# First two projection chunks interleaved in pairs of weight blocks; memory pieces and cross-attention heads turned by transfers, moves of x issued from GpSimd

## What is computed

```python
h = rmsnorm(x, g_mix_pre); proj = h @ w_in             # 2048 x 7168
cb, cc, cv, dq, dk, dv, xq = split(proj)
y_conv  = (cb * causal_dwconv(cc * cv, conv_w)) @ w_conv_out
y_diff  = diff_attention(dq, dk, dv, ...) @ w_diff_out     # 8 heads
k, v    = split(rmsnorm(mem, g_mem) @ w_mem_kv)            # 256 memory tokens
y_cross = (softmax(xq k^T / 16) v) @ w_cross_out           # 4 heads of 256
gates   = sigmoid(h @ w_gate + b_gate)
x = x + rmsnorm((g_a*y_conv + g_b*y_diff + g_c*y_cross) @ w_o, g_mix_post)
u = causal_dwconv(rmsnorm(x, g_ffn_pre) @ w_up, ffn_conv_w)
x = x + rmsnorm((silu(gate) * val) @ w_down, g_ffn_post)
```

## Time and profile before

| | us |
|---|---|
| median of three runs | 1647.38 (1647.07 to 1651.2) |
| profiled execution, its own time | 1648.04 |
| its span, first to last instruction | 1646.3 |
| TensorE busy, whole span | 1634.2 (7301 matmuls) |
| VectorE / ScalarE / GpSimd busy | 1008.9 / 832.4 / 22.7 |
| VectorE: low parts of weight blocks | 690.2 (567 of 1.224) |
| ScalarE: high parts of weight blocks | 597.2 (567 of 1.059) |
| data moved by the 16 DMA engines | 345.13 MB, mean 210 GB/s |

### The profile page before, as it was taken

One profiled execution on the slowest core, in us unless ns is written; L12 is line 12 of the kernel. 1 busy time (PEld: TensorE's weight loads), 2 busy tenths in 40 slices (PEclk: granted clock), 3 DMA queues, 4 the chain that ended last, 5 costly groups with the idle time before them and its releaser, 6 DMA issues.

```text
span 1646.3 us, 22261 instructions
## 1 busy us (share of the span) xinstructions
PE 1634.2 (99%) x7301; PEld 1349.0 (82%) x7301; DVE 1008.9 (61%) x1342; ACT 832.4 (51%) x1056; POOL 22.7 (1%) x53
## 2 busy tenths in 40 slices
PE   9999999999999999999999999999999999999998
PEld 7788888888888888888888888888888888888886
DVE  5565556655566666666655757776766677744544
ACT  6654444444444444444444656666566655543442
POOL 0000000000000000000000000000000000000000
PEclk9999999999999999999999999999999999999999
DMA  7777666777666766676656477777777776755654
GB/s 266 249 220 242 181 174 181 230 215 220 194 198 196 238 207 210 197 235 209 226 197 222 135 227 204 221 219 215 215 222 218 217 220 213 243 192 167 217 193 139
DMA packets 204967, 345.13 MB, mean 210 GB/s; under 512 B 27672, under 2 KB 50537, under 8 KB 204393
## 3 DMA queue, kind: packets, MB, share of 16 engines
q1 hardware_dynamic: 201801, 343.53, 66.9%
q10 hardware_dynamic: 3104, 0.80, 0.2%
HBM read 318.02 MB, written 2.10 MB: 194 GB/s over the span
## 4 chain that ended last, share of the span: by engine, by line
PE 96%; DMA 1%; SPq 1%; DVE 1%; ACT 1%; issue 0%; POOL 0%; DVEq 0%; ACTq 0%; POOLq 0%
PE PS L1408 28%; PE PS L1409 27%; PE PS L1410 27%; PE PS L1535 3%; PE PS L1537 3%; PE PS L1536 3%; PE PS L1573 1%; PE PS L1571 1%; PE PS L1572 1%; DMA raw<-in_w_mem_kv_dram 1%; SPq L334 1%; PE PS L1474 0%; PE PS L1489 0%; DVE w_lo L935 0%; ACT w_hi L578 0%
## 5 line engine op out<-in xcount | busy, mean ns | idle before, releaser
L935 DVE TENSOR_TENSOR w_lo<-raw,w_hi 128x1024 fp32r<-128x1024 f32 x567 | 690.2, 1224 | 562.7 <-ACT w_hi L578 561.4
L578 ACT ACTIVATE w_hi<-raw 128x1024 fp32r<-128x1024 f32 x567 | 597.2, 1059 | 625.8 <-PE PS L1410 529.1
L1408 PE MATMUL PS<-w_hi,hT_hi 128*128 128x512 f32 x1504 | 588.0, 391 | 0.7 <-DVE w_lo L935 0.7
L1410 PE MATMUL PS<-w_hi,hT_lo 128*128 128x512 f32 x1504 | 585.3, 389 | 0.0
L1409 PE MATMUL PS<-w_lo,hT_hi 128*128 128x512 f32 x1504 | 585.2, 389 | 0.0
L1408 PEld LDWEIGHTS PS<-w_hi,hT_hi 128*128 128x128 f32 x1504 | 282.3, 188 | 62.0 <-issue 3.8
L1410 PEld LDWEIGHTS PS<-w_hi,hT_lo 128*128 128x128 f32 x1504 | 282.3, 188 | 59.1
L1409 PEld LDWEIGHTS PS<-w_lo,hT_hi 128*128 128x128 f32 x1504 | 282.3, 188 | 57.9
L1408 PE MATMUL PS<-w_hi,act_hi 128*128 128x512 f32 x336 | 130.9, 390 | 0.0
L1410 PE MATMUL PS<-w_hi,act_lo 128*128 128x512 f32 x336 | 130.7, 389 | 0.0
L1409 PE MATMUL PS<-w_lo,act_hi 128*128 128x512 f32 x336 | 130.7, 389 | 0.0
(11 more groups left out here) (218 smaller groups left out, 1258.3 us busy)
## 6 DMA issues: line engine op xcount, KB each, us to landing
raw<-in_w_up_dram SPq DMA_DIRECT2D x176, 512.0 KB, 4.0
raw<-in_w_in_dram SPq DMA_DIRECT2D x112, 512.0 KB, 4.2
raw<-in_w_gate_dram SPq DMA_DIRECT2D x96, 512.0 KB, 4.5
raw<-in_w_down_dram SPq DMA_DIRECT2D x88, 512.0 KB, 4.1
raw<-in_w_mem_kv_dram SPq DMA_DIRECT2D x32, 512.0 KB, 5.0
raw<-in_w_o_dram SPq DMA_DIRECT2D x32, 512.0 KB, 3.6
up_moved<-up_stage SPq DMA_DIRECT2D x352, 32.0 KB, 2.8
raw<-in_w_conv_out_dram SPq DMA_DIRECT2D x16, 512.0 KB, 3.7
```

The lines of the kernel that those rows point to most:

```text
L578: nc.scalar.activation(w_hi[i % RING][:], raw[i % RING][:], ACT.Copy).then_inc(hi_ready, inc)
L935: nc.vector.tensor_tensor(w_lo[i % RING][:], raw[i % RING][:], w_hi[i % RING][:].bitcast(F32), ALU.subtract).then_inc(lo_ready, inc)
L1408: nc.tensor.matmul(o, a_hi, b_hi, start=first, stop=False)
L1410: last = nc.tensor.matmul(o, a_lo, b_hi, start=False, stop=last_k)
```

## The change

- The blocks of the first two chunks (both memory values) are taken in pairs: blocks 0, 1 of chunk 0, blocks 0, 1 of chunk 1, blocks 2, 3 of chunk 0, and so on. Both accumulators are open at once. Chunk 0 is taken out at step 16 of ScalarE, not 11.
- TensorE turns memory pieces 0 and 1 only. Pieces 2 and 3 are turned like x: ScalarE's copy, 16 transfers, VectorE's transposes. Steps of the six pieces: `COPY_AT`, `TURN_AT`, `HI_AT`, `LO_AT`.
- The 96 transfers for these six pieces are issued by GpSimd (`move_piece`), with the mean square of memory between the second and the third piece. SyncE issues none of them.
- Loads of memory pieces 2 and 3 stand at steps 3 and 4 of SyncE, the constants' at step 6. The sums of squares of memory stand at ScalarE's steps 8 and 10, the constants' copies at VectorE's step 10.
- Cross heads: VectorE writes the normalised probabilities in squares (four instructions), 16 transfers exchange them (eight issued by ScalarE, at its step 7 and step 0 of the next chunk; eight by SyncE at steps 4 and 5 of the next chunk), VectorE transposes inside the squares at step 4 of the next chunk (four instructions), and TensorE multiplies with the values after its block 5 of that chunk, into bank 7. High and low parts follow at step 1 of the chunk after. TensorE's transposes and ScalarE's copy of the turned probabilities are gone.

The diff, cut to its core:

```diff
-    X_COPY = [8, 13, 18, 23]
+    PAIRED = [(c, KB * p + r) for p in range(NCH) for c in range(2) for r in range(KB)]
+    PIECES = [("mem", 2), ("mem", 3)] + [("x", g) for g in range(NCH)]
+    COPY_AT = [3, 5, 10, 14, 18, 22]
+    TURN_AT = [8, 11, 17, 21, 25, 29]
+    HI_AT = [9, 12, 18, 22, 26, 30]
+    LO_AT = [9, 12, 19, 23, 27, 31]
...
+        def chunk_block(c, i):
+
+            return PAIRED[c * CB + i] if c < 2 else (c, i)
...
-            def move_x(g, a):
-
-                if a == 0:
-                    sp.wait_ge(x_copied, g + 1)
-                    if g >= 2:
-                        sp.wait_ge(prep_turned, NCH + g - 1)
+            def move_cross(h, a):
+
+                if a == 2:
+                    sp.wait_ge(x_norm, h + 1)
+                    if h:
+                        sp.wait_ge(x_pT, h)
                 for m in range(P // SQ):
-                    sp.dma_start(x_moved[g % 2][SQ * m:SQ * (m + 1), a, :, :].rearrange("p q n -> p (q n)"),
-                                 x_stage[g % 2][SQ * a:SQ * (a + 1), m, :, :, :].rearrange("p b t n -> p (b t n)")).then_inc(x_moved_in[g % 2], 16)
+                    sp.dma_start(p_moved[SQ * m:SQ * (m + 1), a, :, :].rearrange("p q n -> p (q n)"),
+                                 p_stage[SQ * a:SQ * (a + 1), m, :, :].rearrange("p q n -> p (q n)")).then_inc(x_pT_in, 16)
...
-                        load(c * CB, i, w_mem_kv, i * KB, CROSS + half * CW)
+                        cc, kb = chunk_block(c, i)
+                        load(c * CB, i, w_mem_kv, kb * KB, CROSS + proj[cc][1] * CW)
...
-                    elif c == 0 and i < NCH:
-                        mem_columns(i * CW, (i + 1) * CW, mem_in[i])
-                    for g in range(NCH):
-                        if 0 <= c * CB + i - X_COPY[g] - 5 < P // SQ:
-                            move_x(g, c * CB + i - X_COPY[g] - 5)
...
+                    if 0 <= c - 1 - CROSS_STEP < CH and i in (4, 5):
+                        move_cross(c - 1 - CROSS_STEP, i - 2)
...
-                    if c == 0 and i == NCH + 1:
+                    if c == 0 and i == NCH + 2:
...
+            def move_piece(e):
+
+                pool.wait_ge(x_copied, e + 1)
+                if e >= 2:
+                    pool.wait_ge(prep_turned, 2 + e - 1)
+                for a in range(P // SQ):
+                    for m in range(P // SQ):
+                        pool.dma_start(x_moved[e % 2][SQ * m:SQ * (m + 1), a, :, :].rearrange("p q n -> p (q n)"),
+                                       x_stage[e % 2][SQ * a:SQ * (a + 1), m, :, :, :].rearrange("p b t n -> p (b t n)")).then_inc(x_moved_in[e % 2], 16)
+
+            move_piece(0)
+            move_piece(1)
             pool.wait_ge(squares, 2)
             rms(r_mem[:], sq_mem[:], D)
+            for e in range(2, len(PIECES)):
+                move_piece(e)
...
-                n_end = (c + 1) * CB
+                n_end = (c + 1) * CB + (CB - KB if c == 0 else 0)
...
+                    if c == 2 and i == 0:
+                        after_projection(0)
+                    if i == 3 and c >= 2:
                         after_projection(c - 1)
...
+                    if c * CB + i in COPY_AT:
+                        e = COPY_AT.index(c * CB + i)
+                        what, g = PIECES[e]
+                        act.wait_ge((mem_in if what == "mem" else x_in)[g], 16)
+                        if e >= 2:
+                            act.wait_ge(x_moved_in[e % 2], MOVED * (e // 2))
...
+                    if c == 0 and i == 3:
+                        prepare(1, 1, SCORE_T, gmem_v, memT_hi)
+                    if c == 1 and i in (0, 2):
+                        row_squares(i // 2, mem_sb, sq_mem, i // 2)
+                    if c * CB + i in HI_AT:
+                        e = HI_AT.index(c * CB + i)
...
-                            act.wait_ge(x_pT, h + 1)
-                            nc.scalar.activation(p_crossT[:], PS[:, 7, :].rearrange("p (a b) -> p a b", a=NT), ACT.Copy).then_inc(x_pT_sb, 1)
-                        if i == 7:
-                            act.wait_ge(x_oT, h + 1)
-                            nc.scalar.activation(y_cross_hi[:, 2 * h:2 * h + 2, :],
-                                                 PS[:, 6, :].rearrange("p (a b) -> p a b", a=2), ACT.Copy).then_inc(x_hi, 1)
+                            act.wait_ge(x_norm, h + 1)
+                            if h:
+                                act.wait_ge(x_pT, h)
+                            move_cross(h, 0)
+                    h = c - CROSS_STEP - 1
+                    if 0 <= h < CH:
+                        if i == 0:
+                            move_cross(h, 1)
+                    h = c - CROSS_STEP - 2
+                    if 0 <= h < CH and i == 1:
+                        act.wait_ge(x_oT, h + 1)
+                        nc.scalar.activation(y_cross_hi[:, 2 * h:2 * h + 2, :],
+                                             PS[:, 7, :].rearrange("p (a b) -> p a b", a=2), ACT.Copy).then_inc(x_hi, 1)
...
+                    if c * CB + i in TURN_AT:
+                        e = TURN_AT.index(c * CB + i)
+                        dve.wait_ge(x_moved_in[e % 2], MOVED * (e // 2 + 1))
+                        if e:
+                            dve.wait_ge(prep_lo, 2 * (2 + e))
...
+                                for kb in range(NT):
+                                    last = nc.vector.tensor_scalar(p_stage[:, :, NT * t + kb, :],
+                                                                   p_cross[:, t, kb * P:(kb + 1) * P].rearrange("p (m n) -> p m n", n=SQ),
+                                                                   inv_e[:, 0, t:t + 1], None, ALU.mult)
...
+                    h = c - CROSS_STEP - 1
+                    if 0 <= h < CH:
+                        if i == 4:
+                            dve.wait_ge(x_pT_in, MOVED * (h + 1))
+                            if h:
+                                dve.wait_ge(x_oT, h)
+                            for t in range(NT):
+                                for kb in range(NT):
+                                    last = nc.vector.transpose(p_crossT[:, kb, t * P:(t + 1) * P].rearrange("p (a n) -> p a n", n=SQ),
+                                                               p_moved[:, :, NT * t + kb, :])
+                            last.then_inc(x_pT, 1)
+                    h = c - CROSS_STEP - 2
+                    if 0 <= h < CH and i == 1:
+                        dve.wait_ge(x_hi, h + 1)
...
-                acc = ACC[c % 2]
+                    cc, kb = chunk_block(c, i)
+                    acc = ACC[cc % 2]
+                    if c < 2 or c == NCH:
+                        pe.wait_ge(prep_lo, (0 if c < 2 else 2 * NCH) + kb + 1)
+                    multiply(c * CB, i, CB, memT_hi if on_mem else hT_hi, memT_lo if on_mem else hT_lo, lambda t: acc[:, t, :], kb=kb)
                     if c == 1 and i == 2:
                         pe.wait_ge(const_ready, 3)
-                    if c == 0 and i in (0, 1, 3):
-                        turn_memory((0, 1, 3).index(i) + 1)
+                    if c == 0 and i == 1:
+                        turn_memory(1)
                     if c == 0 and i == CB - 1:
...
-                                pe.wait_ge(x_lo, h)
+                                pe.wait_ge(x_exp, h)
...
-                        if i == 3:
-                            pe.wait_ge(x_norm, h + 1)
+                    h = c - CROSS_STEP - 1
+                    if 0 <= h < CH and i == 5:
+                        pe.wait_ge(x_pT, h + 1)
+                        if h:
+                            pe.wait_ge(x_lo, h)
+                        for db in range(2):
                             for kb in range(NT):
-                                for t in range(NT):
-                                    last = nc.tensor.transpose(PS[:, 7, kb * TOK + t * P:kb * TOK + (t + 1) * P],
-                                                               p_cross[:, t, kb * P:(kb + 1) * P], ident[:])
-                            last.then_inc(x_pT, 1)
-                        if i == 4:
-                            pe.wait_ge(x_pT_sb, h + 1)
-                            for db in range(2):
-                                for kb in range(NT):
-                                    v0 = h * CHD + db * P
-                                    last = nc.tensor.matmul(PS[:, 6, db * TOK:(db + 1) * TOK], mv_tok[:, kb, v0:v0 + P],
-                                                            p_crossT[:, kb, :], start=kb == 0, stop=kb == NT - 1)
-                            last.then_inc(x_oT, 1)
+                                v0 = h * CHD + db * P
+                                last = nc.tensor.matmul(PS[:, 7, db * TOK:(db + 1) * TOK], mv_tok[:, kb, v0:v0 + P],
+                                                        p_crossT[:, kb, :], start=kb == 0, stop=kb == NT - 1)
+                        last.then_inc(x_oT, 1)
```

(26 more changed lines are left out.)

51 lines of the change are left out of this document (11 added, 40 removed).

## The result

The changed kernel takes 1651.17 us (median of 12 runs, 1649.02 to 1652.29); the kernel before took 1648.30 on the same chips (12 runs, 1647.07 to 1651.2). The ratio is 1.0016, 95% interval 1.0009 to 1.0024: 0.16% slower, where 0.33% faster was forecast. The profiled execution took 1651.51, its span 1649.7, 3.4 longer than before.

A forecast was written before the change was run, and what follows sets the result against it. TensorE was taken as the bound. 1648.04 - 1.77 - 1.78 - 2.24 + 0.4 = 1642.65 us, then 0.66 less for the median of earlier runs, gave 1642.0 (0.33% faster); range 1641.0 to 1657.

The forecast's parts named there:

- Bound and views: Whole kernel: TensorE busy 1634.2 of 1646.3 us; time comes only from work taken off it and from its few waits.
- Part 1: Start of the projection loop: memory pieces two and three no longer turned on TensorE, 1.77 us off.
- Part 2: Cross heads: probabilities turned by transfers instead of TensorE transposes, 0.445 us for each of four heads, 1.78 off.
- Part 3: Three TensorE stalls between 64 and 110 us, laid to SyncE's queue of x moves, counted gone whole: 2.24 us off.
- Part 4: First 16 blocks of two chunks interleaved: zero price on TensorE, only due times of memory pieces and chunk 0's evacuation move.
- Part 5: GpSimd issues 96 moves at a taken 0.615 us each: nothing waits, but 0.4 us allowed for piece 2 at block 8.
- signs of being wrong: Profile after: the prediction is wrong if p exceeds 0.73 or starts around the removed transposes lie no closer than before.
- p: GpSimd's time to issue one move, shown by no row before; taken as 0.615 us from SyncE's issue of the same moves.
- Part 6: Cross-head work put on ScalarE, SyncE and VectorE: inside 5.9 us of cover, so zero, bounds 0 and 2 in all.
- The first (GpSimd issues slowly): VectorE's waits for x moves: GpSimd becomes the bound, 1667 us at p = 1.0; chance 0.13 mild, 0.24 hard.
- The second rival: Block 8, block 32 on, cross steps: late chains keep part of the gain, 1642.4 to 1646; chance 0.25 with the third.
- The third: TensorE's stream: stalls stay and only parts 1 and 2 count, 1643.8 us; chance 0.25 together with the second rival.

The follow-up runs named there:

- the first experiment: The changed kernel with the preparation of memory piece 2 one step earlier on ScalarE and VectorE (step 8, not 9): 1646.69 us, 0.9992 of the kernel before.

## Why the prediction was wrong, point by point

**Bound and views.** Right: every gain was on TensorE's stream or in its waits, and where they were was read right.

**Part 1.** Forecast -1.77, measured -1.85 up to block 6.

**Part 2.** Forecast -1.78, measured -1.93 in the changed kernel and alone.

**Part 3.** Forecast -2.24, measured -2.47 (-2.45 alone). SyncE's queue was the cause: with nothing taken from it but the 64 moves, the stalls are gone. None came back behind block 32.

**Part 4.** Zero on TensorE, right: blocks 10 to 16, all interleaved, take 16.32 in both kernels. What it moved were due times, and they are where the change failed.

**Part 5, the failed step.** The issue price was the worry, and it was harmless: 0.50, below the taken 0.615. The due time was right too (32.46, by the trace 32.52), and piece 2's copy was in time (first issue at 15.8, 15.2 taken). Two other steps were wrong, and both are the same oversight: I followed only piece 2's own chain, and not the weight blocks that stand ahead of it in the queues.

First the turn. By the prediction's terms it ends at 29.6 (15.2, 16 issues at 0.615, a landing of 3.1, 1.42); it ended at 31.86. The landing, taken as 3.1 from the earlier trace rows, is 5.8 in the median up to 40 us (4.6 to 7.1):

```profile
DMA to landing us min/median/max: 4.6/5.8/7.1
```

The rows of before come from 37 us on, and the early stretch, in which weights, memory, constants and x all are on their way, was priced by them. Yet the long landing cost only the 0.27 for which VectorE waited: its turn stands behind the low part of block 8, done at 30.17. With the 1.9 that the first experiment shows from the turn's end to block 8, an estimate, TensorE would have started at 33.8, 1.2 late. Second and larger, the remaining 2.4: piece 2's preparation stands behind the split of block 9 in ScalarE's program, and so waits for a load that TensorE does not need for another block. The prediction asked this of VectorE's queue for x, but not of ScalarE's and VectorE's for the memory. "ScalarE's splits wait for nothing new" was the false sentence: they wait for their weights, and those had more in front of them. 1.6 "at worst" was 3.67, and behind it came 2.83 at half clock, which no term had. Of the prediction's signs of being wrong (p over 0.73, starts no closer) neither came; the one that did was a wait over 0.5 on TensorE.

**The sum.** A term was missing altogether: GpSimd's drain, 3.0. No row of before could give its size, but its closing DRAIN of 48 ns and the end of SyncE's outputs 4.9 behind it were there to be read; they say that up to 4.9 of a longer drain would be hidden, and that a longer one would not.

**Part 6.** Zero, right. The cross heads' moves cost nothing, alone or beside the rest.

**The rivals.** The first (GpSimd issues slowly) was wrong in its mechanism: p is 0.50. It was the reason for the range's upper end, so that 1651.17 lies inside the range is luck. (Its prices start once from 1641.6 and once from 1642.0; nothing rests on it.) The Trainium skill, page "DMA: Bandwidth & Descriptors", section "Latency and other measured facts", puts the first byte of a transfer issued by GpSimd at about 1 us, against 600 ns for SyncE or ScalarE. The runs show no first byte; from issue to landing the shortest are 1.9 from GpSimd and 2.0 from SyncE, and GpSimd's time per issue was 0.50, not 1. The second rival (piece 2 late at block 8) named the right place with the wrong price, 1.6 against 3.67 and the clock's 2.83. The third did not occur.

**The forecast's number.** 1642.0 is what the change gives with SyncE's order and the last norms mended (1642.1 to 1642.3). The gains were sized right; the prediction was wrong in what they set off.

## What to carry to other kernels

When a transfer takes over work from the bounding engine at the start of a program, price its landing by rows of that stretch, with all that is then in flight, and follow every engine that must touch the result: what is written ahead of that touch in program order, and which load does that wait for. A wait of 2 to 4 us on TensorE can cost nearly as much again in clock; filler matmuls in an unused bank cap that loss, while an earlier load removes it. If GpSimd issues transfers and has work at the end of the program, look at its closing drain, and give that last work to another engine.

## What the runs showed of the hardware that I had not expected

- GpSimd's closing drain grows with the transfers that it issued over the whole program: 0.048 us at none, 0.138 at one, 5.290 at 64, 7.903 at 96, 0.082 each. It does so even when the last of them was issued 1560 us earlier (79.0 against 1641.6). It begins when GpSimd's program ends, at 934.7 in the run where that has no more work, and is hidden there.
- GpSimd's issue of a 32 KB move takes 0.496 us, SyncE's 0.590, ScalarE's 0.612 (the cross heads' moves).
- TensorE's granted clock fell to 1.2 GHz behind waits of 3.5, 2.05 and 1.70 us, stayed at 2.4 GHz behind 1.9 us in the profiled execution of one kernel, and behind 0.79 in another. So the length of the wait alone did not decide it. In the longest case the low clock lasted 6.8 us (from the shares of the windows above).
- A 512 KB weight load took 6.7 us from issue to landing in the kernel before and 12.2 in the changed one (block 9), 8.1 with SyncE's order mended.
- 14 float32 matmuls of 128x128 are 28 records, 0.11 us apart at full clock.
